# A diffusion block on one core: its first-stage matrix products in four-byte floats on two column tiles, and identity products between them

## What is computed

```
mod = silu(c) @ ada_w + ada_b                 # six vectors of 2048 for the latents
sh1, sc1, g1, sh2, sc2, g2 = split(mod, 6)    # the same for the context, from c_ctx
h  = rms_norm(x,   norm1_g) * (1 + sc1)  + sh1
hc = rms_norm(ctx, norm1_g) * (1 + csc1) + csh1
proj = h @ w_in;  proj_c = hc @ w_in[:, :N_QKV]
a = neighbourhood_attention(qa, ka, va, ...);  b = diff_attention(qb, kb, vb, ...)
x = x + g1 * ((sigmoid(ga) * (a @ w_pa) + sigmoid(gb) * (b @ w_pb)) @ w_out)
x = x + g2 * conv_ffn(rms_norm(x, norm2_g) * (1 + sc2) + sh2)
out = rms_norm(x)
```

## Time and profile before

| | us |
|---|---|
| median of 3 runs | 1785.69 (1784.96 to 1789.5) |
| the profiled execution | 1786.11 |
| its span, first to last instruction | 1784.4 |
| mean granted clock of TensorE | 0.988 of full speed |

### The profile page before, as it was taken

The page is one execution under the profiler, slowest core; times in us unless marked ns, Lnnn a source line. Parts: engine busy times, 40 slices in busy tenths (PEclk is TensorE's granted clock), DMA queues, the critical chain, the costliest instruction groups (busy, mean ns, idle before and its releaser), DMA issues.

```text
span 1784.4 us, 23637 instructions
## 1 busy us (share of the span) xinstructions
PE 1726.9 (97%) x8631; PEld 1437.7 (81%) x8631; DVE 1165.5 (65%) x1446; ACT 817.0 (46%) x1013; POOL 105.2 (6%) x155
## 2 busy tenths in 40 slices
PE   5999999999999999999999999999999999999996
PEld 3678888887888758888888888888888888888885
DVE  5888776878774795545545576666666666645556
ACT  6774222542222465444444465555555555544443
POOL 0002221123220000000000000000000000000000
PEclk7999999999999999999999999999999999999998
DMA  9889887649884405555655545655555555555551
GB/s 351 305 306 327 306 279 252 212 129 338 295 271 148 154 1 200 178 190 191 193 190 211 190 143 189 189 189 190 189 190 190 189 188 188 188 189 195 192 194 65
DMA packets 160716, 369.30 MB, mean 207 GB/s; under 512 B 11471, under 2 KB 12127, under 8 KB 159758
## 3 DMA queue, kind: packets, MB, share of 16 engines
q1 hardware_dynamic: 140352, 296.18, 49.5%
q0 software_dynamic: 19728, 72.04, 12.0%
q10 hardware_dynamic: 574, 0.25, 0.0%
HBM read 366.26 MB, written 2.16 MB: 206 GB/s over the span
## 4 chain that ended last, share of the span: by engine, by line
PE 87%; DVE 6%; DMA 3%; ACT 1%; issue 1%; SPq 0%; POOL 0%; DVEq 0%; POOLq 0%; ACTq 0%
PE ps L1655 20%; PE ps L1654 10%; PE ps L1664 10%; PE ps L1666 10%; PE ps L1665 10%; PE ps L1966 4%; PE ps L1967 4%; PE ps L1968 4%; PE ps L1566 3%; PE ps L1568 2%; PE ps L1567 2%; DMA ada_raw<-in_ada_w 2%; PE ps L1557 2%; DVE w_lo L957 1%; PE ps L1651 1%
## 5 line engine op out<-in xcount | busy, mean ns | idle before, releaser
L957 DVE TENSOR_TENSOR w_lo<-raw,w_hi 128x1024 fp32r<-128x1024 f32 x552 | 669.1, 1223 | 484.5 <-ACT w_hi L569 483.4
L569 ACT CAST w_hi<-raw 128x1024 fp32r<-128x1024 f32 x552 | 575.2, 1049 | 879.2 <-PE ps L1666 335.5
L1655 PE MATMUL ps<-h2T,w_hi 128*128 128x512 f32 x1320 | 462.5, 394 | 0.0
L1654 PE MATMUL ps<-h2T,w_lo 128*128 128x256 f32 x1320 | 366.5, 278 | 0.0
L1655 PEld LDWEIGHTS ps<-h2T,w_hi 128*128 128x128 f32 x1320 | 247.5, 188 | 53.6
L1654 PEld LDWEIGHTS ps<-h2T,w_lo 128*128 128x128 f32 x1320 | 247.9, 188 | 4.0
L1664 PE MATMUL ps<-w_hi,hT 128*128 128x512 f32 x512 | 200.7, 392 | 0.0
L1666 PE MATMUL ps<-w_hi,hT 128*128 128x512 f32 x512 | 199.4, 389 | 0.0
L1665 PE MATMUL ps<-w_lo,hT 128*128 128x512 f32 x512 | 199.2, 389 | 0.0
L1029 DVE SCALAR_TENSOR_TENSOR ada_acc<-ada_raw,silu_c,ada_acc 128x512 f32<-128x512 f32 x240 | 180.1, 751 | 27.0 <-DMA ada_raw<-in_ada_w 8.9
L1966 PE MATMUL ps<-w_hi,f_hi 128*128 128x512 f32 x352 | 137.0, 389 | 1.0 <-DVE conv_in L1396 1.0
(11 more groups left out here) (215 smaller groups left out, 2056.6 us busy)
## 6 DMA issues: line engine op xcount, KB each, us to landing
raw<-in_ffn_w_up SPq DMA_DIRECT2D x176, 512.0 KB, 4.3
raw<-in_w_in SPq DMA_DIRECT2D x160, 512.0 KB, 4.7
ada_raw<-in_ada_w POOLq DMA_DIRECT2D x128, 512.0 KB, 5.9
raw<-in_ffn_w_down SPq DMA_DIRECT2D x88, 512.0 KB, 3.5
raw<-in_ada_w SPq DMA_DIRECT2D x64, 512.0 KB, 5.6
raw<-in_w_out SPq DMA_DIRECT2D x32, 512.0 KB, 3.6
raw<-in_w_branch_a SPq DMA_DIRECT2D x16, 512.0 KB, 3.5
raw<-in_w_branch_b SPq DMA_DIRECT2D x16, 512.0 KB, 3.5
```

The lines of the kernel that those rows point to most:

```text
L569: act.copy(w_hi[:, s % SPLIT_SLOTS, :], raw[:, s, :]).then_inc(hi_ready[s], 1)
L957: dve.tensor_tensor(w_lo[:, s % SPLIT_SLOTS, :], raw[:, s, :], w_hi[:, s % SPLIT_SLOTS, :], ALU.subtract).then_inc(lo_ready[s], 1)
L1654: pe.matmul(ps[:, b + t, 0:SEQ], w_lo[:, row4(s), at], high(kc), start=False, stop=False)
L1655: mm = pe.matmul(o, w_hi[:, row4(s), at], both(kc), start=False, stop=(kc == KC - 1))
```

## The change

- An ada unit is no longer rounded and split. TensorE multiplies `raw` itself, in float32, with the pairs of silu values in `c_pair` as the stationary operand. There are 32 stationary columns, of which two are the pair. One matmul writes the first 512 columns of the unit to the partitions 0 to 31 of a bank, the other the second 512 to the partitions 32 to 63 of the same bank: two column tiles. A quarter needs one bank, and quarter 2 has bank 5 for itself.
- SyncE loads a slot again once TensorE has multiplied the ada unit in it (`ada1_used`). The tokens are loaded after unit 3, the context after unit 7.
- ScalarE and VectorE round and split only the eight k units of the head, and the loops over units are replaced by a plain order of steps.
- The sums of a quarter are two rows of 512 columns on each tile; they are turned by four transposes instead of eight, and no addition of two parts is needed.
- TensorE multiplies the identity by itself (`keep_busy`, into bank 7): six times before the first transpose, six times after it, and twelve times each after the units 3 and 7.
- The numbers of the jobs go down by eight, with no effect but on the counts that are waited for.

The diff, cut to what the prediction speaks of (declarations, the removed lists of hand-placed steps and unchanged context left out):

```diff
@@ -63,11 +63,11 @@
...
-JOB_NA = 8
-JOB_DIFF = 14
-JOB_MERGE = 20
-JOB_OUT = 32
-JOB_UP = 36
+JOB_NA = 0
+JOB_DIFF = 6
+JOB_MERGE = 12
+JOB_OUT = 24
+JOB_UP = 28
...
@@ -89,16 +89,29 @@
...
-ADA_BANKS = (0, 4, 4, 4)
+ADA_BANKS = (0, 4, 5, 4)
+PIECES = 2
+PIECE = UNIT // PIECES
+PIECE_AT = [32 * n for n in range(PIECES)]
...
+def ada_before(u):
+    return sum(kind == "ada" for kind, *_ in HEAD[:u])
+def loads_before(j, s):
+    return HEAD.index(("k", s)) // SLOTS if isinstance(j, int) and j == 0 else len(HEAD) // SLOTS - 1 + j
...
-ADA_JOBS = [9, 9, 10, 10, 11, 11, 12, 13, 14, 14, 15, 15, 16, 16, 17, 17]
+ADA_JOBS = [1, 1, 2, 2, 3, 3, 4, 5, 6, 6, 7, 7, 8, 8, 9, 9]
...
@@ -436,22 +448,30 @@
...
+                slot, last = u % SLOTS, u - SLOTS
+                if last >= 0 and HEAD[last][0] == "ada":
+                    sp.wait_ge(ada1_used, ada_before(last) + 1)
...
-                    load(u // SLOTS, u % SLOTS, shift_scale[:, kc, :, GROUP * q:GROUP * (q + 1)])
+                    if last >= 0 and HEAD[last][0] == "k":
+                        sp.wait_ge(lo_ready[slot], 1)
+                    sp.dma_start(raw[:, slot, :].rearrange("p (a n) -> p a n", a=2),
+                                 shift_scale[:, kc, :, GROUP * q:GROUP * (q + 1)]).then_inc(raw_landed[slot], 16)
...
-                    load(u // SLOTS, u % SLOTS, w_in_v[:, 2 * s:2 * s + 2, KA:KA + GROUP])
-                if u == 5:
+                    load(0, s, w_in_v[:, 2 * s:2 * s + 2, KA:KA + GROUP])
+                if u == 3:
...
-                if u == 8:
+                if u == 7:
...
+                    if n == 1 and s == 0:
+                        sp.wait_ge(ada1_used, ada_before(len(HEAD)))
...
@@ -560,7 +580,7 @@
...
-                act.wait_ge(raw_landed[s], 16 * j + 16)
+                act.wait_ge(raw_landed[s], 16 * loads_before(j, s) + 16)
...
@@ -601,11 +621,10 @@
...
-                act.wait_ge(used[u % SLOTS], u // SLOTS + 1)
+                act.wait_ge(ada1_used, ada_before(u) + 1)
...
-                act.copy(mod_rows[:, q % 2, :].rearrange("p (a n) -> p a n", a=2), ps[0:4, b:b + 2, :])\
-                    .then_inc(mod_rows_ready, 1)
+                act.copy(mod_rows[:, q % 2, :], ps[0:PIECE_AT[-1] + 2, b, 0:PIECE]).then_inc(mod_rows_ready, 1)
...
@@ -632,54 +651,28 @@
...
-            for u in range(len(HEAD) + 2):
-                round_hi(u // SLOTS, u % SLOTS)
-                if u == 1:
-                    act.wait_ge(lam_step, 2)
-                    act.activation(lam[:], lam[:], ACT.Exp).then_inc(lam_exp, 1)
-                    warm_up(ACT.Sqrt)
-                if u == 6:
-                    act.wait_ge(tokens_landed, 16)
...
-                for q in range(QUARTERS):
-                    kc, since = SHARE * q, u - ENDS[q]
-                    if q == 0:
-                        if since == 6:
-                            modulate(kc)
-                        if since == 7:
-                            modulate(kc + 1)
-                        if since == 9:
-                            modulate(kc + 2)
-                        if since == 12:
-                            modulate(kc + 3)
-                    elif q < QUARTERS - 1:
-                        if since == 4:
...
+            act.wait_ge(lam_step, 2)
+            act.activation(lam[:], lam[:], ACT.Exp).then_inc(lam_exp, 1)
+            warm_up(ACT.Sqrt)
+            for st in range(2):
+                act.wait_ge((tokens_landed, ctx_landed)[st], 16)
+                square_tokens(2 * st)
+                square_tokens(2 * st + 1)
+                root1(st)
+            for q in range(QUARTERS):
+                if q:
+                    round_hi(0, 2 * q - 1)
+                read_mod_rows(q)
+                if q == QUARTERS - 1:
+                    round_hi(0, 2 * q)
+                for kc in range(SHARE * q, SHARE * q + 2):
+                    modulate(kc)
+                round_hi(0, 2 * q + 1 if q == QUARTERS - 1 else 2 * q)
+                for kc in range(SHARE * q + 2, SHARE * q + 4):
+                    modulate(kc)
+            for s in range(2):
+                round_hi(1, s)
...
@@ -976,31 +969,26 @@
...
-            for st in range(2):
-                part = c_parts[:, 0:4 * KC].rearrange("p (k f) -> p f k", f=4)
-                step(dve.tensor_copy(part[:, 2 * st, :], silu_c[:, st * KC:(st + 1) * KC]))
-                dve.tensor_tensor(part[:, 2 * st + 1, :], silu_c[:, st * KC:(st + 1) * KC], part[:, 2 * st, :],
-                                  ALU.subtract).then_inc(c_ready, 1)
+            dve.tensor_copy(c_pair[:, 0:2 * KC].rearrange("p (k s) -> p s k", s=2),
+                            silu_c[:].rearrange("p (s k) -> p s k", s=2)).then_inc(c_ready, 1)
+                sums = ps[:, MOD_BANK, 0:64 * SHARE].rearrange("p (b m a w) -> p m w a b", m=2, a=PIECES // 2, w=32)
-                else:
-                    dve.wait_ge(mod1_step, 2 * q)
-                dve.tensor_reduce(mod_sums[:], ps[:, MOD_BANK, 0:8 * SHARE].rearrange("p (n s f) -> p n s f", s=2, f=2),
-                                  AX.X, ALU.add).then_inc(mod_cols_summed, 1)
-                dve.wait_ge(mod_cols_summed, q + 1)
-                dve.tensor_tensor(gain1[:, :, at], both(1), spread(V_ADAB + KC), ALU.add).then_inc(mod1_step, 1)
-                dve.tensor_tensor(shift1[:, :, at], both(0), spread(V_ADAB), ALU.add).then_inc(mod1_step, 1)
+                dve.tensor_tensor(by_piece(gain1[:, :, at]), sums[:, 1, 0:2], by_piece(spread(V_ADAB + KC)), ALU.add)\
+                    .then_inc(mod1_step, 1)
+                dve.tensor_tensor(by_piece(shift1[:, :, at]), sums[:, 0, 0:2], by_piece(spread(V_ADAB)), ALU.add)\
+                    .then_inc(mod1_step, 1)
...
@@ -1072,71 +1060,43 @@
...
-            for u in range(len(HEAD) + 2):
-                split_lo(u // SLOTS, u % SLOTS)
...
-                for q in range(QUARTERS):
-                    kc, since = SHARE * q, u - ENDS[q]
-                    if q == 0:
-                        if since == 3:
-                            modulation1(q)
-                        if since == 6:
-                            split_modulated(kc)
-                        if since == 7:
-                            split_modulated(kc + 1)
-                        if since == 9:
...
+            mean_square1(0)
+            inverse_root1(0)
+            norm_tokens(0)
+            norm_tokens(1)
...
+            for q in range(QUARTERS):
+                if q:
+                    split_lo(0, 2 * q - 1)
+                if q == QUARTERS - 1:
+                    split_lo(0, 2 * q)
+                modulation1(q)
+                for kc in range(SHARE * q, SHARE * q + 2):
+                    split_modulated(kc)
+                split_lo(0, 2 * q + 1 if q == QUARTERS - 1 else 2 * q)
+                for kc in range(SHARE * q + 2, SHARE * q + 4):
+                    split_modulated(kc)
+            for s in range(2):
+                split_lo(1, s)
...
@@ -1518,11 +1478,18 @@
...
+            def keep_busy(n):
+                for _ in range(n):
+                    pe.matmul(ps[:, 7, 0:P], ident, ident, start=True, stop=True)
...
+            keep_busy(6)
...
-            pe.wait_ge(c_ready, 2)
+            keep_busy(6)
+            pe.wait_ge(c_ready, 1)
...
@@ -1543,21 +1510,23 @@
...
-                for n in range(2 * SHARE):
-                    mm = pe.transpose(ps[:, MOD_BANK, 4 * n:4 * n + 4], mod_rows[:, q % 2, n * P:(n + 1) * P],
-                                      consts[0:4, 0:4])
+                rows = PIECE_AT[-1] + 2
+                for n in range(PIECE // P):
+                    mm = pe.transpose(ps[:, MOD_BANK, 32 * PIECES * n:32 * PIECES * n + rows],
+                                      mod_rows[:, q % 2, n * P:(n + 1) * P], consts[0:rows, 0:rows])
...
-                if kc == 0 and q:
-                    pe.wait_ge(mod_rows_ready, q)
-                for half in range(2):
-                    for w in (w_hi, w_lo):
-                        mm = pe.matmul(ps[:, ADA_BANKS[q] + half, :], c_parts[:, 4 * kc:4 * kc + P],
-                                       w[:, row4(u % SLOTS), half * GROUP:(half + 1) * GROUP],
-                                       start=(kc == 0 and w is w_hi), stop=(kc == KC - 1 and w is w_lo))
-                return mm
+                slot = u % SLOTS
+                if kc == 0 and q == QUARTERS - 1:
+                    pe.wait_ge(mod_rows_ready, q - 1)
+                pe.wait_ge(raw_landed[slot], 16 * (u // SLOTS) + 16)
+                for n, at in enumerate(PIECE_AT):
+                    mm = pe.matmul(ps[at:at + 32, ADA_BANKS[q], 0:PIECE], c_pair[:, 2 * kc:2 * kc + 32],
+                                   raw[:, slot, n * PIECE:(n + 1) * PIECE], start=(kc == 0), stop=(kc == KC - 1))
+                mm.then_inc(ada1_used, 1)
...
@@ -1576,8 +1545,7 @@
...
-                    take(u // SLOTS, u % SLOTS)
-                    mm = unit_ada(u, *unit)
```

(32 more changed lines are left out.)

93 lines of the change are left out of this document (10 added, 83 removed).

## The result

The changed kernel takes 1777.59 us (median of 6 runs, 1773.98 to 1781.68), the kernel before, in runs beside it, 1788.36 (6 runs, 1784.96 to 1790.27). The ratio is 0.9943, with a 95% interval of 0.9929 to 0.9957: 10.2 us less (the medians by themselves differ by 10.8). The forecast was 1776.0 and -9.7 us. The profiled execution took 1778.22 us with a span of 1776.5; for the kernel before the two are 1786.11 and 1784.4, so the spans differ by 7.9.

A forecast was written before the change was run, and what follows sets the result against it. Ahead of k0 bytes and the steps after landing bound the head, then almost only TensorE. -8.5 - 2.2 + 2.8 - 3.8 + 2.0 = -9.7 us from 1786.1 gives 1776.4, less 0.4 to the median: 1776.0; range 1768 to 1800.

The forecast's parts named there:

- Part 1: Head up to k0: set by bytes landing, then cast and split; k0 starts at 54.1 instead of 62.64, -8.5 us.
- The identity matmuls: Ahead of k0, in TensorE's waits for tokens: their use is the clock; costed at nothing, at most 2 x 5.2 us.
- Parts 2 and 3: From k0 on: 40 ada units at 0.90 instead of 0.954 us, -2.2; 28 tile-shape switches at 0.1 us, +2.8.
- Part 4: From k0 on: TensorE's waits for late w_lo go, as VectorE has two splits a quarter instead of 18, -3.8 us.
- Part 5: Slots free only after TensorE's multiplication, so five k units' load, cast and split each wait 0.4 us, +2.0 us.
- Behind the head: After the head's end, taken as 157.3 us in the kernel before: the change costs nothing there.
- (A): Ada units: tile overlap real but poor, 1.06 us a unit; -3.3 us in all, 1782.4 us; chance 0.14.
- (B): Ada units: tiles don't overlap, 1.72 us a unit, or stretches held at 1.2 GHz; +25.7 us, 1811; chance 0.20.
- (C): From k0 on: no switches and no new waits, 1770 us; chance 0.66 together with the forecast.

The follow-up runs named there:

- e8: The changed kernel run once more, with nothing altered: 1776.85 us, ratio 0.9941 to the kernel before.
- e2: The kernel before with only the 36 identity matmuls added: 1787.17 us, ratio 0.9997 to the kernel before.
- e1: The changed kernel without its 36 identity matmuls: 1775.12 us, ratio 0.9934 to the kernel before.
- e10: e9 without the identity matmuls: 1767.88 us, ratio 0.9889 to the kernel before.
- e4: The changed kernel with four column tiles of 256 columns instead of two of 512: 1781.09 us, ratio 0.9968 to the kernel before.
- e5: The changed kernel with four column tiles and every k unit loaded three units earlier: 1773.98 us, ratio 0.9912 to the kernel before.
- e6: The changed kernel, still with two column tiles, with every k unit loaded three units earlier: 1774.75 us, ratio 0.9928 to the kernel before.
- e3: The changed kernel with both halves of an ada unit on the same column tile, in two banks: 1816.71 us, ratio 1.0157 to the kernel before.
- e11: The kernel before, keeping all casts and splits and its hand-placed order, with TensorE multiplying raw on two tiles, no identity matmuls: 1788.08 us, ratio 1.0006.
- e9: e5 with k6 and k7 loaded last, only k0 to k5 three units early: 1768.18 us, ratio 0.9893 to the kernel before.
- e12: e9 with two column tiles instead of four: 1775.99 us, ratio 0.9935 to the kernel before.

## Why the prediction was right

The mechanism and the sum held: -9.7 forecast, -10.2 measured. Its parts did not all hold, and some of them cancelled. Part 1 brought 1.5 us less than forecast and the switches cost 1.0 more; against that the unit brought 1.6 more, the stalls 1.4 more, and the new wait cost nothing instead of 2.0. By these parts the head should have been 12.2 us shorter, and the profiles show 12.4 (the first) and 10.8 (e8). That the total came out within 0.5 us is in part luck.

**Part 1, `k0`: -8.5 forecast, -7.0 in the profile.** The bound was named rightly: the chain shows the load, the cast and the split of `k0`, and from the landing to the first matmul it takes 55.63 - 53.19 = 2.44 us, as forecast (2.5). The landing was forecast at 51.6 and came at 53.19. The rate was a little better than assumed (395 GB/s), so the bytes were wrong: 19.07 MB had moved by then, by the count of the changed kernel's transfers up to 53.19 us, not 18.2.

```profile
DMA packets 8819, 19.07 MB, mean 359 GB/s; under 512 B 657, under 2 KB 1313, under 8 KB 8306
...
raw<-in_ada_w SPq DMA_DIRECT2D x31, 512.0 KB, 10.3
```

31 ada units had been issued, not the 24 ahead of `k0`: the seven behind it were already taking their share of the engines. The step that failed is "the order of the loads puts 25 units ... before `k0`"; an order of issue is not an order of landing. 0.87 MB at 395 GB/s are 2.2 us, less 0.4 for the better rate; 1.8, where the landing was 1.6 later than forecast.

**The identity matmuls: nothing, as costed.** "Their use is the clock" was right, and the clock was worth nothing there: e2 leaves room for a gain of at most 0.12%, and e1 and e10 show none.

**Parts 2 and 3, the unit and the switches: +0.6 forecast, 0.0 found.** The unit in a stream is 0.86, not 0.90: the forecast's 0.90 held some of the switch already. So the unit gives 40 x (0.86 - 0.954) = -3.8. The switches are fewer than forecast and dearer. There are 24 from `k0` to `k5` and not 28: of the ten groups of transposes only seven stand between ada units (the forecast had nine), two stand between a k unit and an ada unit, one inside `k0`. In the two timelines, from start to start, each of the 12 ada stretches takes 0.12 more than its units (4.42 - 5 x 0.86 in the chain above). A group of transposes behind one takes 0.58 or 0.59, where the kernel before has 0.36 when nothing is waited for; the two groups behind a k unit take 0.53. The k units take 28.7 us in all instead of 28.3. That makes 12 x 0.12 + 7 x 0.225 + 2 x 0.18 + 0.4 = 3.8 us, 0.16 a switch, where the forecast took 0.1 for each. The Trainium skill says that a change of tiling mode drains TensorE (TensorEngine Tiling, Key Properties), without a duration. The trace agrees that a switch costs something, and the forecast's estimate by that rule, 0.16 a switch, gives 3.8 for 24. A group of transposes between ada units in the kernel before, by its timeline:

```profile
73.45 0.60 PE L1537 MATMUL ps<-consts,tokens 128*128 128x128 f32 x4
73.81 0.48 PE L1557 MATMUL ps<-w_hi,c_parts 128*128 128x512 f32 x1
```

**Part 4, VectorE's stalls: -3.8 forecast, about -5.2.** The forecast found 1.9 us in each of two of the five intervals. Over all five, the kernel before has 28.32 us of k units, 40 units of 0.954 (38.16), ten groups of transposes of 0.36 (3.60) and two `turn_mod` (1.16), 71.2 of the 76.0: 4.8 us of stalls and small losses, not 3.8. `turn_mod` got 0.2 shorter each time, with four transposes for eight, 0.4 that the forecast left out. Together -5.2, and the unit and the switches add nothing; measured -5.2.

**Part 5, the new wait: +2.0 forecast, 0 found.** In the changed kernel TensorE waits for `w_lo` only once up to 160 us, ahead of `k0`:

```profile
PE ps L1527 <- DMA raw<-in_ada_w: 8.1, 9, 2.8
PE ps L1535 <- DVE w_lo L950: 2.5, 1, 2.5
```

The bounds of 0 to 1.5 for each wait held the value, but at their end. e4 shows that the mechanism is real and close: at half the unit's price it costs 15.4 us in six waits, and e5 and e6 show that an earlier load takes it away.

**Behind the head: 0 forecast, +4.5 in this profile, +0.6 in e8's.** Since the same program shows both, most of it is not the change. Whether a little of it is can't be told from single profiles, of which two of one program differ by 3.9 us. The median difference (-10.2) stands between the head's -12.4 and the span's -7.9.

**The rivals.** (A), 1.06 a unit: fell, the overlap is complete. The Trainium skill has 2.38 for three column tiles (TensorE: Matmul & The Clock Gate, Measured speedup vs the span model); scaled to a pair as an estimate that is 1.08 a unit, above the 0.86 that the trace shows. (B), no overlap: not what happened, but e3 built it, and its price was right in size: 1811 forecast, 1816.7 measured, `k0` at 58.7 forecast and 62.06 measured. Its first half was too kind (and its landing of the context at 27.7 works out to 27.5); the half from `k0` to `k5` grew by 105.54 - 70.78 = 34.8 over the changed kernel, where 40 x 0.856 = 34.2 are the units. That the narrow ada stretches would hold the clock down fell as well: the granted clock is 1.00 from `k0` to `k5`. (C), 1770 without switches and waits: the switches were there, the waits not.

## What to carry to other kernels

A float32 product with few stationary columns can skip the rounding and splitting if its column tiles overlap: four float32r matmuls became two float32 matmuls side by side at 0.86 a unit against 0.954, and two other engines lost 136.5 us of work. The multiplication by itself gave nothing (e11), and without the overlap of the tiles the rest was a loss (e3): the gain came from what the two other engines had held up. When the units of a stage get cheaper, load the few that still need a cast and a split earlier by what those steps take, and only as long as others don't need the slot sooner: against the kernel before, four cheap tiles gave 7 us with late loads (e4), 14 with all k units pulled forward (e5) and 20 with the last two left in place (e9); with two tiles the same order gave nothing over the change itself (e12). Filling TensorE's gaps to raise its clock was worth nothing here, where bytes set the end of the stretch (e1, e2, e10).

## What the runs showed of the hardware

- Two float32 column tiles of 32 columns run wholly in parallel: 0.43 us from pair to pair of records (0.86 a unit). Over a stretch of five units, the switch included, it is 0.884 a unit, while the same two matmuls on one tile take 1.74 (e3). Four tiles of 256 columns take 1.93 us for four units.
- The 24 switches between a column-tiled stream and full-size work cost some 3.8 us from `k0` to `k5`, 0.16 each on average.
- The bytes issued ahead of a load don't alone set its landing: with seven more loads issued behind it, 19.07 MB had moved when `k0` landed, where 18.2 lay ahead of it, some 2.2 us at 395 GB/s.
- The granted clock can differ between two executions of one program at the same place: 0.50 and 1.00 from 1030 to 1034 us. The rest behind the head differs by 3.9 us between the two profiles of the changed kernel, over a third of what the change is worth, so a single profile can't carry a statement of that size.
